# A hybrid attention and state-space layer on one core: one gate product moved into the states, the second FFN's opening reordered, head projections in two banks

## The chip, the core and the metric

The kernel runs on one core of a Trainium2 chip, as one launch. The metric is the device time of that launch in microseconds (us). Five engines work side by side, each through its own list of instructions in order: TensorE (PE, matmuls and transposes), VectorE (DVE), ScalarE (ACT), GpSimd (POOL), and SyncE (SP), which here does nothing but issue transfers. They are held together by semaphores that the code writes out by hand. PSUM, where TensorE writes, has eight banks of 128 x 512 float32.

## The reference

```python
h = h + 0.5 * swiglu(rmsnorm(h, ffn1_norm), ffn1_w_gate, ffn1_w_up, ffn1_w_down)
n = rmsnorm(h, mix_norm)
z = n @ w_in          # c_q 256 | c_kv 128 | k_rope 32 | u 512 | g_attn 1024 | g_ssm 1024
q  = rmsnorm(c_q) @ w_uq ; kv = rmsnorm(c_kv) @ w_ukv        # 8 heads: 64 + 32 rotary, values 64
attn = softmax(q k^T / sqrt(96)) v                           # bidirectional
y = S5_forward(u) + S5_backward(u) + D * u                   # 32 groups of 16, 64 complex states
glu = gelu(y) @ w_glu + b_glu ; ssm = glu[:, :512] * sigmoid(glu[:, 512:])
h = h + (sigmoid(g_attn) * (attn @ w_o_attn) + sigmoid(g_ssm) * (ssm @ w_o_ssm)) @ w_out
h = h + 0.5 * swiglu(rmsnorm(h, ffn2_norm), ffn2_w_gate, ffn2_w_up, ffn2_w_down)
out = rmsnorm(h, final_norm)
```

There are 1,024 tokens, the model is 1,024 wide and each FFN 2,816; all inputs are float32.

## The kernel before, in words

**Three passes.** Every large product is made of float32 operands split in a high and a low part. `three_passes` (L46 to L50) issues high x high (L48), low x high (L49) and high x low (L50) into one bank. So each operand needs a high part (a cast, mostly on ACT) and a low part (raw minus high, on DVE or POOL) before its product can begin.

**Phases.** The kernel runs through phases: first FFN (to about 720 us), projections out of `w_in` (to 836), state-space part (837 to 1068), GLU (to about 1180), attention (to 1512), merge (to 1669), second FFN (to the end at 2354). Inside a phase each engine has one block of code, written in order by hand; there is no scheduler.

**State-space phase** (`ssm_phase`). PE turns `u` (32 transposes, L1628), then makes the state inputs: 16 quads of 8 matmuls (`states`, L1638), whose banks ACT empties with two copies each (L1673, L1674, semaphore `ec`). It then makes the products within a chunk, 8 quads of 4 matmuls (`within`, L1647), with a matrix M (called `ss_C_mat` in the profile, as is everything in that space) loaded from `kern_dram`. DVE adds them to `u` (L1728, `wadd`), where POOL had multiplied `u` by the diagonal D (L1714). DVE then scans 127 steps over the states (L1735 to L1739) while PE makes gate products: `side.gp.product(pe, n)`, 16 of them in two groups, 48 matmuls each, from a tile of `w_in` (`ga_raw`, two buffers), its high part on ACT (L156) and its low part on POOL (L164). `GATES_FIRST` of them stand ahead of the outputs of the scan. SP loads tile n+2 of the gates only when the low part of tile n is done, and it stands in SP's list behind the load of the output matrix `C_dram` (4 MB), which waits for the last `within`.

**GLU phase.** PE turns y (L1814), ACT and DVE split it in two (`gl_yT_hi`, `gl_yT_lo` L1849), eight half tiles counted by `s_lo`. `glu.product(pe, n)` multiplies by the GLU weights, whose low parts (`glu_lo`, L164) DVE makes in between.

**Attention phase.** For a block g of 128 queries PE turns the probabilities of block g-2 in two parts (`turn`, L2020), makes the scores of block g, and, in some blocks, part 0 or 1 of the values (`values`, L2039 and L2040, bank `pv_out` = 6), the turned inverses (`inverses`, L2029, bank `inv_out` = 7), and one of the four projections of the next head (`project(n, x)`: x = 0, 1 the two halves of the queries, 6 products; x = 2, 3 the keys, 3 products). Projections come in the blocks 0, 1, 4, 5 of a head, behind everything else of their block. For the values of a pair of blocks J, ACT copies the upper half out of bank 6 (`at_spread` L2120) and DVE adds the lower half (L2208, semaphore `sum`); DVE then multiplies by the inverses (`scale`). In before all projections of heads 1 to 7 use bank 7. DVE's rows of a block come in this order: low part of turn 0 (L2202), maximum of the scores (L2191), low part of turn 1 (L2202), the sum (L2208) and its product (L2213), then the projection's rotary or low parts (L2181, L2182 or L2184).

**Second FFN** (`ffn_phase` with `ahead`). The residual is in `rows` (8 row tiles). ACT and DVE turn it into `f_B_hi` and `f_B_lo`; DVE multiplies the rows by their statistics and gain in place (L1039) once the store of the unscaled row to `kept` has read it. The weights come as raw tiles (L789); ACT makes the high part (L918), DVE the low part (L1023). POOL adds up raw tiles (L1289) and rows (L1272 to L1277) for the checks' sums, which PE turns (L1303, `turn_sums`).

Of the kernel before, what the change touches and what calls it, by code (L numbers as in the profile page):

```python
# [17 lines left out]
ALU = mybir.AluOpType  # L18
# [14 lines left out]
P = 128  # L33
# [653 lines left out]
def ffn_phase(nc, tag, gain, w_gate, w_up, w_down, rows, ident, psum, hidden, residual, x=None, finish=None, tables=None, ahead=0, following=None):  # L687
# [10 lines left out]
    with Phase(nc) as ctx:  # L698
# [85 lines left out]
        def _(sp):  # L784
# [24 lines left out]
            if ahead:  # L809
                load_matrix(0)  # L810
            take(0)
            take(1)
            sp.dma_start(gb[:], gain.rearrange("(a d) -> a d", a=1).broadcast_to([P, D])).then_inc(s_gain, 16)
# [4 lines left out]
            for m in range(QUAD, ST):  # L818
                take(m)
# [206 lines left out]
        def _(dve):  # L1026
# [57 lines left out]
            if ahead:  # L1084
                normalised(2)
# [6 lines left out]
            lows_low(3)  # L1092
            normalised(3)
# [489 lines left out]
def ssm_phase(nc, w, rows, rows_at, ident, psum, nT_hi, nT_lo, u, gates, kern_dram, C_dram, lam8_dram):  # L1583
# [5 lines left out]
    with Phase(nc) as ctx:  # L1589
# [18 lines left out]
        @block.sync  # L1608
        def _(sp):
            for t in range(T):  # L1610
                at = (T - 1 - t) * SG
                sp.dma_start(M[t * SG:(t + 1) * SG], kern_dram[:, :, at:at + P]).then_inc(s["m"], 16)
            sp.dma_start(Db, w["ssm_d"][0:1, :].rearrange("a (g i) -> a g i", i=SG).broadcast_to([P, GROUPS, SG])).then_inc(s["d"], 16)
            side.gp.load(sp, 0)
            side.gp.load(sp, 1)
            sp.dma_start(lam8[:].rearrange("p a b g -> p (a b g)"), lam8_dram).then_inc(s["lam"], 16)
            sp.wait_ge(s["within"], NQ)
            sp.wait_ge(s["ud"], NQ)
            sp.dma_start(C_mat[:], C_dram.rearrange("c p g x -> p c g x")).then_inc(s["c"], 16)
            side.sync(sp)  # L1620

        @block.tensor
        def _(pe):
# [16 lines left out]
            for q in range(2 * NQ):  # L1640
                states(q)
            pe.wait_ge(s["m"], 16 * T)
            for q in range(NQ):
                if q >= 4:
                    pe.wait_ge(s["wadd"], q - 3)
                for g in range(4 * q, 4 * q + 4):
                    mm = pe.matmul(psum[:, q % 4, g % 4 * P:(g % 4 + 1) * P], UT[:, g, :], M[:, g, :], start=True, stop=True)  # L1647
                mm.then_inc(s["within"], 1)
            pe.wait_ge(s["wadd"], NQ)
            for n in range(GATES_FIRST):  # L1650
                side.gp.product(pe, n)
# [16 lines left out]
        def _(act):  # L1668
# [9 lines left out]
            side.gp.high(act, 1)  # L1678
            for q in range(NQ, 2 * NQ):
                state(q)  # L1680

# [26 lines left out]
        @block.gpsimd  # L1708
        def _(pool):
            pool.wait_ge(s["d"], 16)  # L1710
            for q in range(NQ):
                pool.wait_ge(s["ut"], q + 1)
                g = slice(4 * q, 4 * q + 4)
                pool.tensor_tensor(u[:, g], u[:, g], Db[:, g].unsqueeze(2).broadcast_to([P, 4, T, SG]), ALU.mult).then_inc(s["ud"], 1)  # L1714
            for n in range(side.N):
                side.gp.low(pool, n)

        @block.vector
        def _(dve):
# [4 lines left out]
            for q in range(NQ):  # L1724
# [3 lines left out]
                dve.tensor_tensor(u[:, g], psum[:, q % 4, :].rearrange("p (g t i) -> p g t i", g=4, i=SG), u[:, g], ALU.add).then_inc(s["wadd"], 1)  # L1728
# [38 lines left out]
def glu_phase(nc, w, ident, psum, y, gates, partial):  # L1767

    with Phase(nc) as ctx:
# [38 lines left out]
        def _(pe):  # L1808
# [7 lines left out]
            pe.wait_ge(s_lo, NT)  # L1816
            for n in range(glu.N):
                glu.product(pe, n)
# [57 lines left out]
def attention_phase(nc, w, ident, psum, rows_at, latent_rows, trig_rows, aT_hi, aT_lo):  # L1876

    with Phase(nc) as ctx:
# [42 lines left out]
        job_bank = lambda n, x: psum[:, x if n == 0 else 7, :]  # L1921
# [46 lines left out]
        def _(pe):  # L1968
# [6 lines left out]
            def project(n, x):  # L1975
# [9 lines left out]
                elif n:  # L1985
                    pe.wait_ge(s["proj_act"], job)
                    pe.wait_ge(s["proj_dve"], job)
                    if n >= 2 and x in (0, 2):
                        pe.wait_ge(s["scale"], 2 * n - 3 + x // 2)
# [42 lines left out]
            def values(J, part):  # L2032

                if part == 0:
                    pe.wait_ge(s["tr_lo"], (4 * J + 4) * PARTS)
                    if J:
                        pe.wait_ge(s["sum"], J)
                for k in range(4 * part, 4 * part + 4):
# [491 lines left out]
```

## Time and profile before

| | |
|---|---|
| Median of three runs | 2366.19 us (2361.04 to 2367.4) |
| Profiled execution | 2355.74 us, its span 2354.0 us |
| Mean granted TensorE clock | 0.964 of full speed |
| PE busy | 2160.3 us (92% of the span) |
| DVE busy | 1489.9 us (63%) |
| ACT busy | 917.3 us (39%) |
| POOL busy | 592.3 us (25%) |
| Transfers | 263.52 MB, 112 GB/s over the span |

The span runs from the first to the last instruction of the core; the profiled execution lies 10.45 us under the median of the runs. Times inside a profile are us from the span's start.

### The profile page before, as it was taken

To read this page: it belongs to the slowest core of one execution; us is meant where nothing else is said; L and a number is where in the kernel's file an instruction comes from. 1 tells how busy PE (TensorE), PEld (TensorE's weight loads), DVE (VectorE), ACT (ScalarE), POOL (GpSimd) and SP (SyncE) were. 2 spreads that over 40 slices of the span, in tenths; PEclk is the share of its full clock that TensorE was granted. 3 is DMA by queue.
4 is the path that set the end of the run, shared out by engine and by line. 5 is a ranking of instruction groups with operands and counts; after the bars stand their busy time and mean duration, and the time that the engine had idled before them with its cause. 6 is when DMAs were issued, how large, how long until landed. Compare 5 with 4: busy or idle time off the path is not lost. (4 is left out here: it accounts for less than half of the span.)

```text
span 2354.0 us, 27672 instructions
## 1 busy us (share of the span) xinstructions
PE 2160.3 (92%) x10074; PEld 1789.2 (76%) x10074; DVE 1489.9 (63%) x2322; ACT 917.3 (39%) x1552; POOL 592.3 (25%) x494
## 2 busy tenths in 40 slices
PE   5999999999997979998959898699799999999997
PEld 4778888878886978886747776577678888887886
DVE  7786676657776229942357777462765655656777
ACT  5423333324453241153137776322333333223444
POOL 5347777810000022220012222000433333320000
PEclk8999999999998989998979999799899999999999
DMA  4424343376333264322420000163222324339433
GB/s 125 113 82 132 114 141 117 95 296 220 99 116 129 68 112 149 90 72 76 139 58 7 4 6 1 58 246 125 90 85 85 117 90 126 95 102 366 125 98 109
DMA packets 234615, 263.52 MB, mean 112 GB/s; under 512 B 34736, under 2 KB 169392, under 8 KB 233968
## 3 DMA queue, kind: packets, MB, share of 16 engines
q1 hardware_dynamic: 234480, 261.75, 35.0%
q8 instruction: 81, 1.33, 0.2%
q14 instruction: 54, 0.44, 0.1%
HBM read 185.13 MB, written 76.58 MB: 111 GB/s over the span
## 5 line engine op out<-in xcount | busy, mean ns | idle before, releaser
L48 PE MATMUL psum<-f_B_hi,f_A_hi 128*128 128x512 f32 x1232 | 487.1, 395 | 35.6 <-DVE f_B_lo L1051 22.7
L50 PE MATMUL psum<-f_B_hi,f_A_lo 128*128 128x512 f32 x1232 | 481.8, 391 | 0.0
L49 PE MATMUL psum<-f_B_lo,f_A_hi 128*128 128x512 f32 x1232 | 481.8, 391 | 0.0
L48 PEld LDWEIGHTS psum<-f_B_hi,f_A_hi 128*128 128x128 f32 x1232 | 232.8, 189 | 87.0 <-issue 30.1
L50 PEld LDWEIGHTS psum<-f_B_hi,f_A_lo 128*128 128x128 f32 x1232 | 232.6, 189 | 49.3
L49 PEld LDWEIGHTS psum<-f_B_lo,f_A_hi 128*128 128x128 f32 x1232 | 233.0, 189 | 47.0
L1289 POOL TENSOR_TENSOR f_S<-f_raw 128x512 f32<-128x512 f32 x88 | 131.0, 1489 | 470.4 <-DVE f_A_lo L1023 289.9
L918 ACT CAST f_A_hi<-f_S 128x512 fp32r<-128x512 f32 x176 | 109.3, 624 | 347.7 <-PE psum L50 339.7
L48 PE MATMUL psum<-f_wd,f_hh 128*128 128x512 f32 x616 | 240.6, 391 | 3.6 <-DVE f_wd L1068 3.6
L50 PE MATMUL psum<-f_wd,f_hh 128*128 128x512 f32 x616 | 240.3, 390 | 0.0
L49 PE MATMUL psum<-f_wd,f_hh 128*128 128x512 f32 x616 | 240.2, 390 | 0.0
L952 ACT CAST f_hh<-f_h_raw 128x512 fp32r<-128x512 f32 x154 | 96.0, 624 | 240.4 <-PE psum L50 231.7
L1023 DVE TENSOR_TENSOR f_A_lo<-f_raw,f_A_hi 128x512 fp32r<-128x512 f32 x132 | 135.3, 1026 | 68.0 <-ACT f_A_hi L918 67.3
L1066 DVE TENSOR_TENSOR f_hh<-f_h_raw,f_hh 128x512 fp32r<-128x512 f32 x154 | 106.5, 692 | 104.9 <-ACT f_hh L952 104.1
L1023 DVE TENSOR_TENSOR f_A_lo<-f_S,f_A_hi 128x512 fp32r<-128x512 f32 x176 | 140.1, 798 | 2.5 <-ACT f_A_hi L918 1.3
L48 PEld LDWEIGHTS psum<-f_wd,f_hh 128*128 128x128 f32 x616 | 116.0, 188 | 28.7 <-DVE f_wd L1068 4.4
L50 PEld LDWEIGHTS psum<-f_wd,f_hh 128*128 128x128 f32 x616 | 116.0, 188 | 24.2
L49 PEld LDWEIGHTS psum<-f_wd,f_hh 128*128 128x128 f32 x616 | 116.1, 188 | 23.9
L918 ACT CAST f_A_hi<-f_raw 128x512 fp32r<-128x512 f32 x132 | 81.8, 621 | 127.0 <-PE psum L50 127.0
L2202 DVE TENSOR_TENSOR at_PT_lo<-psum,at_PT_hi 128x512 fp32r<-128x512 f32 x128 | 87.8, 687 | 65.6 <-ACT at_PT_hi L2098 65.4
L1068 DVE TENSOR_TENSOR f_wd<-f_wd_raw,f_wd 128x512 fp32r<-128x512 f32 x154 | 105.7, 686 | 0.0
L1714 POOL TENSOR_TENSOR u<-u,ss_C_mat 128x512 f32<-128x512 f32 x8 | 9.8, 1268 | 375.4 <-DMA ss_C_mat<-ssm_d 375.4
(327 smaller groups left out, 4308.9 us busy)
## 6 DMA issues: line engine op xcount, KB each, us to landing
f_h_raw<-hidden SPq DMA_DIRECT2D x154, 256.0 KB, 2.7
hidden<-rows SPq DMA_DIRECT2D x44, 768.0 KB, 4.5
f_raw<-ffn_w_gate SPq DMA_DIRECT2D x44, 512.0 KB, 5.2
f_raw<-ffn_w_up SPq DMA_DIRECT2D x44, 512.0 KB, 5.1
f_wd_raw<-ffn_w_down SPq DMA_DIRECT2D x44, 512.0 KB, 9.1
rows<-x SPq DMA_DIRECT2D x16, 512.0 KB, 7.1
ga_raw<-w_in SPq DMA_DIRECT2D x16, 512.0 KB, 4.3
gates<-ga_sig SPq DMA_DIRECT2D x32, 256.0 KB, 2.2
```

The lines of the kernel that those rows point to most:

```text
L48: pe.matmul(out, lhs_hi, rhs_hi, start=first, stop=False, skip_group_check=go_on)
L49: pe.matmul(out, lhs_hi, rhs_lo, start=False, stop=False, skip_group_check=go_on)
L50: return pe.matmul(out, lhs_lo, rhs_hi, start=False, stop=last, skip_group_check=go_on)
L918: act.copy(A_hi[:, q], src).then_inc(s_hi, 1)
L952: act.copy(hh[v % 2][0][:], h_raw[v % 8][:]).then_inc(s_dhi, 1)
L1023: eng.tensor_tensor(A_lo[:, q], src, A_hi[:, q].bitcast(F32), ALU.subtract).then_inc(s_lo, 1)
L1066: dve.tensor_tensor(hh[v % 2][1][:], h_raw[v % 8][:], hh[v % 2][0][:].bitcast(F32), ALU.subtract).then_inc(s_dlo, 1)
L1068: dve.tensor_tensor(wd[v % 2][1][:], wd_of(q, k), wd[v % 2][0][:].bitcast(F32), ALU.subtract).then_inc(s_dlo, 1)
L1289: pool.tensor_tensor(S[:, i], a, b, op).then_inc(s_sum, 1)
L1714: pool.tensor_tensor(u[:, g], u[:, g], Db[:, g].unsqueeze(2).broadcast_to([P, 4, T, SG]), ALU.mult).then_inc(s["ud"], 1)
L2202: dve.tensor_tensor(pt(PT_lo, g, x), turned_bank(x), pt(PT_hi, g, x).bitcast(F32), ALU.subtract).then_inc(s["tr_lo"], 1)
```

## The change

Four places are edited. **State-space:** the first gate product moves between the last `states` and the first `within`; the `within` products take banks 4 to 7 instead of 0 to 3; SP loads gate tile 0 and D ahead of M; ACT casts tile 1 only after all states; POOL makes the low part of tile 0 after six of its eight multiplications by D. **GLU:** the first product no longer waits for all eight low half tiles, but inside its passes for two more at each k. **Second FFN:** SP stores rows 4 and 5 before it loads the first gate tile, and DVE scales rows 4 and 5 only after the low parts of the first tile. **Attention:** the projections use bank 6 for x = 0, 2 and bank 7 for x = 1, 3; they wait for the emptying of the projection before the last one (`job - 1`) instead of the last; x = 0, 2 wait for `sum` (the bank of the values) where they waited for `scale`, x = 1, 3 for `scale`; and the values wait for projections that had to be waited for by the inverses alone.

```diff
@@ -806,16 +806,18 @@
                     sp.dma_start(residual[m * P:(m + 1) * P, :], rows[:, m, :]).then_inc(s_kept[m], 16)
-            if ahead:
-                load_matrix(0)
             take(0)
             take(1)
+            if ahead:
+                take(QUAD)
+                take(QUAD + 1)
+                load_matrix(0)
             sp.dma_start(gb[:], gain.rearrange("(a d) -> a d", a=1).broadcast_to([P, D])).then_inc(s_gain, 16)
...
                 load_matrix(0)
-            for m in range(QUAD, ST):
+            for m in range(QUAD + ahead // 2, ST):
                 take(m)
@@ -1082,7 +1084,8 @@
             if ahead:
-                normalised(2)
+                variance(2)
+                rstd(2)
             lows_low(1)
@@ -1090,6 +1093,9 @@
             lows_low(3)
+            if ahead:
+                scaled(QUAD)
+                scaled(QUAD + 1)
             normalised(3)
@@ -1607,11 +1613,11 @@
         def _(sp):
+            side.gp.load(sp, 0)
+            sp.dma_start(Db, w["ssm_d"][0:1, :].rearrange("a (g i) -> a g i", i=SG).broadcast_to([P, GROUPS, SG])).then_inc(s["d"], 16)
             for t in range(T):
...
                 sp.dma_start(M[t * SG:(t + 1) * SG], kern_dram[:, :, at:at + P]).then_inc(s["m"], 16)
-            sp.dma_start(Db, w["ssm_d"][0:1, :].rearrange("a (g i) -> a g i", i=SG).broadcast_to([P, GROUPS, SG])).then_inc(s["d"], 16)
-            side.gp.load(sp, 0)
             side.gp.load(sp, 1)
@@ -1639,15 +1645,18 @@
                 states(q)
+            side.gp.product(pe, 0)
             pe.wait_ge(s["m"], 16 * T)
             for q in range(NQ):
-                if q >= 4:
+                if q < 4:
+                    pe.wait_ge(s["ec"], 2 * (2 * NQ - 3 + q))
+                else:
                     pe.wait_ge(s["wadd"], q - 3)
                 for g in range(4 * q, 4 * q + 4):
-                    mm = pe.matmul(psum[:, q % 4, g % 4 * P:(g % 4 + 1) * P], UT[:, g, :], M[:, g, :], start=True, stop=True)
+                    mm = pe.matmul(psum[:, 4 + q % 4, g % 4 * P:(g % 4 + 1) * P], UT[:, g, :], M[:, g, :], start=True, stop=True)
                 mm.then_inc(s["within"], 1)
             pe.wait_ge(s["wadd"], NQ)
-            for n in range(GATES_FIRST):
+            for n in range(1, GATES_FIRST):
                 side.gp.product(pe, n)
@@ -1675,9 +1684,9 @@
             side.gp.high(act, 0)
-            side.gp.high(act, 1)
             for q in range(NQ, 2 * NQ):
                 state(q)
+            side.gp.high(act, 1)

@@ -1709,10 +1718,12 @@
             for q in range(NQ):
+                if q == NQ - 2:
+                    side.gp.low(pool, 0)
                 pool.wait_ge(s["ut"], q + 1)
...
                 pool.tensor_tensor(u[:, g], u[:, g], Db[:, g].unsqueeze(2).broadcast_to([P, 4, T, SG]), ALU.mult).then_inc(s["ud"], 1)
-            for n in range(side.N):
+            for n in range(1, side.N):
                 side.gp.low(pool, n)
@@ -1725,7 +1736,7 @@
                 dve.wait_ge(s["within"], q + 1)
-                dve.tensor_tensor(u[:, g], psum[:, q % 4, :].rearrange("p (g t i) -> p g t i", g=4, i=SG), u[:, g], ALU.add).then_inc(s["wadd"], 1)
+                dve.tensor_tensor(u[:, g], psum[:, 4 + q % 4, :].rearrange("p (g t i) -> p g t i", g=4, i=SG), u[:, g], ALU.add).then_inc(s["wadd"], 1)
             dve.wait_ge(s["lam"], 16)
@@ -1813,9 +1824,8 @@
                 mm.then_inc(s_t, 1)
-            pe.wait_ge(s_lo, NT)
             for n in range(glu.N):
-                glu.product(pe, n)
+                glu.product(pe, n, (lambda k: pe.wait_ge(s_lo, 2 * k + 2)) if n == 0 else None)
             for n in range(KT):
@@ -1918,7 +1928,7 @@
         v_bank = lambda m: psum[:, 4 + m % 4, :]
-        job_bank = lambda n, x: psum[:, x if n == 0 else 7, :]
+        job_bank = lambda n, x: psum[:, x if n == 0 else 6 + x % 2, :]
         inv_out = psum[0:VH, 7, :]
@@ -1983,9 +1993,11 @@
                 elif n:
-                    pe.wait_ge(s["proj_act"], job)
-                    pe.wait_ge(s["proj_dve"], job)
+                    pe.wait_ge(s["proj_act"], job - 1)
+                    pe.wait_ge(s["proj_dve"], job - 1)
                     if n >= 2 and x in (0, 2):
+                        pe.wait_ge(s["sum"], 2 * n - 3 + x // 2)
+                    if n >= 2 and x in (1, 3):
                         pe.wait_ge(s["scale"], 2 * n - 3 + x // 2)
@@ -2035,6 +2047,8 @@
                         pe.wait_ge(s["sum"], J)
+                    pe.wait_ge(s["proj_act"], min(2 * JOBS + 2 * J, HEADS * JOBS))
+                    pe.wait_ge(s["proj_dve"], min(2 * JOBS + 2 * J, HEADS * JOBS))
                 for k in range(4 * part, 4 * part + 4):
```

What this does to the order of the instructions is seen on three engines. First PE in the state-space phase, before: `u` turned, the states (L1638), the products within a chunk (L1647), and then the gates' first product.

```order
L1628 MATMUL psum<-ident,u 128x128 x32
L1638 MATMUL psum<-ss_UT,rows 128x128 x64
L1647 MATMUL psum<-ss_C_mat,ss_UT 128x128 x32
L48 MATMUL psum<-nT_hi,ga_hi 128x512
L49 MATMUL psum<-nT_lo,ga_hi 128x512
L50 MATMUL psum<-nT_hi,ga_lo 128x512
```

The same place of the changed kernel (the three gate rows come 16 times before L1656; L1634, L1644 and L1656 are before's L1628, L1638 and L1647).

```order
L1634 MATMUL psum<-ident,u 128x128 x32
L1644 MATMUL psum<-ss_UT,rows 128x128 x64
L48 MATMUL psum<-nT_hi,ga_hi 128x512
L49 MATMUL psum<-nT_lo,ga_hi 128x512
L50 MATMUL psum<-nT_hi,ga_lo 128x512
L1656 MATMUL psum<-ss_C_mat,ss_UT 128x128 x32
```

One gate product of 48 matmuls has moved ahead of the 32 matmuls within a chunk. On SP the loads of that phase stand in before in this order (M is `kern_dram`, D is `ssm_d`):

```order
L1612 DMA ss_C_mat<-kern_dram 16x32x128 x8
L1613 DMA ss_C_mat<-ssm_d 128x512
L148 DMA ga_raw<-w_in 128x8x128 x2
L1616 DMA ss_lam<-lam_dram 128x128
L1619 DMA ss_C_mat<-C_dram 128x2x4096
L148 DMA ga_raw<-w_in 128x8x128
L1558 DMA gates<-ga_sig 128x512 x2
```

And in the changed kernel:

```order
L148 DMA ga_raw<-w_in 128x8x128
L1617 DMA ss_C_mat<-ssm_d 128x512
L1620 DMA ss_C_mat<-kern_dram 16x32x128 x8
L148 DMA ga_raw<-w_in 128x8x128
L1622 DMA ss_lam<-lam_dram 128x128
L1625 DMA ss_C_mat<-C_dram 128x2x4096
L148 DMA ga_raw<-w_in 128x8x128
L1564 DMA gates<-ga_sig 128x512 x2
```

Gate tile 0 and D have moved to the front; gate tile 2 (the single load behind `C_dram`) has kept its place. Second, PE in the attention phase, with what each row waits for. The profile's names of semaphores are shared between phases: `f1_gain` is here the attention's `sum`, `f1_x_in2` its `scale`, `f1_x_in5` its `tr_lo`, and `tb_kr` and `tb_xt` are `proj_act` and `proj_dve`. Before, for x = 0, x = 1 and the first values behind them:

```order
L2020 MATMUL psum<-ident,at_prob 128x128 x3
L48 MATMUL psum<-at_lT_hi,at_w_hi 128x512 [waits tb_kr,f1_x_in2,tb_xt,tb_x]
...
L48 MATMUL psum<-at_lT_hi,at_w_hi 128x512 [waits tb_kr,tb_xt]
...
L2039 MATMUL psum<-at_PT_hi,at_V 128x512 [waits f1_gain,f1_x_in5]
```

And in the changed kernel:

```order
L2032 MATMUL psum<-ident,at_prob 128x128 x3
L48 MATMUL psum<-at_lT_hi,at_w_hi 128x512 [waits tb_kr,f1_gain,tb_xt,tb_x]
...
L48 MATMUL psum<-at_lT_hi,at_w_hi 128x512 [waits f1_x_in2,tb_kr,tb_xt]
...
L2053 MATMUL psum<-at_PT_hi,at_V 128x512 [waits tb_xt,tb_kr,f1_gain,f1_x_in5]
```

No instruction has moved; x = 0 waits for `sum` instead of `scale`, x = 1 has `scale` added, and the values wait for the projections' emptying too. Third, DVE at the start of the second FFN, before:

```order
L1039 SCALAR_TENSOR_TENSOR rows<-rows,f_stat,f_gb 128x1024 x2
L1051 TENSOR_TENSOR f_B_lo<-psum,f_B_hi 128x4x128 x2
L1023 TENSOR_TENSOR f_A_lo<-f_raw_16682,f_A_hi 128x512 x2
L1051 TENSOR_TENSOR f_B_lo<-psum,f_B_hi 128x4x128 x4
L359 TENSOR_SCALAR f_stat<-f_stat 128x2
```

In the changed kernel:

```order
L1053 TENSOR_TENSOR f_B_lo<-psum,f_B_hi 128x4x128 x2
L1025 TENSOR_TENSOR f_A_lo<-f_raw_16733,f_A_hi 128x512 x2
L1053 TENSOR_TENSOR f_B_lo<-psum,f_B_hi 128x4x128 x4
L1041 SCALAR_TENSOR_TENSOR rows<-rows,f_stat,f_gb 128x1024 x2
L359 TENSOR_SCALAR f_stat<-f_stat 128x2
```

The two scalings of rows 4 and 5 have moved behind all low parts of the first tile.

## Rows read from the trace of the kernel before

**Rows 1.** The page, part 1: busy us, share of span, instructions.

```profile
PE 2160.3 (92%) x10074; PEld 1789.2 (76%) x10074; DVE 1489.9 (63%) x2322; ACT 917.3 (39%) x1552; POOL 592.3 (25%) x494
```

**Rows 2.** Timeline, PE, 836 to 892: start, length, instructions [idle <-releaser].

```profile
865.48 5.50 PE L1638 MATMUL psum<-ss_UT,rows 128*128 128x128 f32 x32 [12.10 <-ACT ss_H L1674]
...
878.98 0.50 PE L48 MATMUL psum<-nT_hi,ga_hi 128*128 128x512 f32 x1 [0.85 <-DVE u L1728]
```

**Rows 3.** Timeline of ACT, then POOL; transfers, 837 to 900 (us to landing).

```profile
861.65 1.05 ACT L156 CAST ga_hi<-ga_raw 128x1024 fp32r<-128x1024 f32 x1 [9.49 <-DMA ga_raw<-w_in]
...
893.91 2.39 POOL L164 TENSOR_TENSOR ga_lo<-ga_raw,ga_hi 128x1024 fp32r<-128x1024 f32 x1 [19.52 <-ACT ga_hi L156]
...
ss_C_mat<-C_dram SPq DMA_DIRECT2D x1, 4096.0 KB, 13.1
```

**Rows 4.** Timeline of PE, then DVE, in the GLU phase.

```profile
1084.25 0.79 PE L48 MATMUL psum<-gl_yT_hi,glu_hi 128*128 128x512 f32 x1 [5.05 <-DVE gl_yT_lo L1849]
...
1082.16 2.03 DVE L1849 TENSOR_TENSOR gl_yT_lo<-psum,gl_yT_hi 128x512 fp32r<-128x512 f32 x2
```

**Rows 5.** Waits, 1235 to 1560: us in total, times, longest.

```profile
PE psum L2020 <- DVE at_PT_lo L2202: 20.5, 14, 3.7
...
PE psum L48 <- DVE at_qf L2182: 4.6, 6, 0.8
PE psum L48 <- DVE at_KT_lo L2184: 4.6, 6, 0.8
```

**Rows 6.** Timeline of PE, then DVE, one head of the attention.

```profile
1325.47 0.48 PE L48 MATMUL psum<-at_lT_hi,at_w_hi 128*128 128x512 f32 x1
...
1330.13 0.47 PE L48 MATMUL psum<-at_lT_hi,at_w_hi 128*128 128x512 f32 x1 [0.78 <-DVE at_qf L2182]
...
1333.85 0.48 PE L2039 MATMUL psum<-at_PT_hi,at_V 128*128 128x512 f32 x1
...
1342.49 0.47 PE L48 MATMUL psum<-at_lT_hi,at_w_hi 128*64 128x512 f32 x1
...
1348.76 0.63 PE L2020 MATMUL psum<-ident,at_prob 128*128 128x128 f32 x4 [1.47 <-DVE at_PT_lo L2202]
...
1327.05 0.67 DVE L2208 TENSOR_TENSOR at_spread<-psum,at_spread 64x512 f32<-64x512 f32 x1
...
1333.98 0.69 DVE L2182 SCALAR_TENSOR_TENSOR at_qf<-psum,at_trig 32x512 f32<-32x512 f32 x1
...
1344.17 0.67 DVE L2208 TENSOR_TENSOR at_spread<-psum,at_spread 64x512 f32<-64x512 f32 x1
```

**Rows 7.** Timeline of PE, DVE and POOL, start of the second FFN.

```profile
1691.45 0.77 PE L48 MATMUL psum<-f_B_hi,f_A_hi 128*128 128x512 f32 x1 [14.98 <-DVE f_B_lo L1051]
...
1680.70 3.64 DVE L1039 SCALAR_TENSOR_TENSOR rows<-rows,f_stat,f_gb 128x1024 f32<-128x1024 f32 x2 [3.36 <-DMA kept<-rows]
...
1685.47 3.44 DVE L1023 TENSOR_TENSOR f_A_lo<-f_raw,f_A_hi 128x512 fp32r<-128x512 f32 x2
...
1697.74 0.69 DVE L1023 TENSOR_TENSOR f_A_lo<-f_raw,f_A_hi 128x512 fp32r<-128x512 f32 x1
...
1683.23 2.25 POOL L1272 TENSOR_TENSOR f_T_A_lo<-rows 128x512 f32<-128x512 f32 x1
```

**Rows 8.** Timeline of PE: stalls of 2.2 to 2.65 us elsewhere.

```profile
54.98 0.50 PE L48 MATMUL psum<-f_B_hi,f_A_hi 128*128 128x512 f32 x1 [2.65 <-DVE f_A_lo L1023]
...
1671.12 5.34 PE L1303 MATMUL psum<-ident,rows 128*128 128x128 f32 x32 [2.20 <-PEq L63]
...
1715.78 0.79 PE L48 MATMUL psum<-f_B_hi,f_A_hi 128*128 128x512 f32 x1 [2.65 <-DVE f_A_lo L1023]
```

**Rows 9.** Windows: us, then busy (count) of five engines, PEclk, DMA share, GB/s.

```profile
879.00:890.00 11.00, 11.00 (x48) 9.09 (x49) 9.66 (x40) 0.00 (x0) 0.00 (x0) 1.00 0.98 391
1084.20:1094.90 10.70, 10.65 (x40) 8.53 (x41) 0.00 (x0) 1.62 (x2) 0.00 (x0) 0.85 0.04 10
1671.20:1672.20 1.00, 1.00 (x5) 1.00 (x6) 0.00 (x0) 0.00 (x0) 0.00 (x0) 0.50 0.07 13
```


## The prediction

> **What bounds the kernel now.** I read the page first, then the timeline of PE around each edited place, then what DVE, ACT and POOL did there. PE is busy 92% of the span [rows 1] and the edits add or remove no matmul, so the change is worth what it does to PE's stalls and, through them, to PE's clock. Before, the edited places hold these stalls: 12.10 us in the states, for ACT [rows 2], which itself stood 9.49 us for the first gate tile's load because that was queued behind M [rows 3]; 5.05 us ahead of the first GLU product [rows 4]; 14.98 us at the start of the second FFN [rows 7]; and in each head of the attention 0.77 us at x = 1 and 0.77 at x = 3, which wait for the emptying of the one bank (4.6 us over 6 heads each [rows 5]), and 1.47 us at a turn just after x = 3, six times the same [rows 6]. That is 3.0 us of stalls a head: PE bounds the heads too.
>
> **State-space.** Gate tile 0 now comes first, so ACT casts it right behind its first eight quads (it was free from 861.65 - 9.49 = 852.2) and PE's states end near 859.7 instead of 870.98: ACT's eight last quads no longer wait for the tile. PE then has the product of 48 matmuls, which took 11.0 us [rows 9], to fill the time until M has landed and POOL's multiplications are done. Their place is where the stall of 12.1 us was. `within` then begins at 870.6 as before (it took the 8.0 us from 870.98 to 878.98 with DVE's last addition [rows 2]), so `C_dram`'s load and the scan are issued when they were. What follows is one product shorter: product 1 starts at 878.98 and ends at 889.9. Here is what is late next. Tile 2's load has kept its place behind the 4 MB of `C_dram`, which took 13.1 us to land, and its low part ended at 893.91 + 2.39 = 896.3 [rows 3]; nothing in that chain moves. Before, product 2 had its turn only at 900.8 and hid it. Now PE waits 6.4 us for it, and comes back at the low clock: 40 matmuls after the 5.05 us stall took 10.70 us at a mean granted clock of 0.85, where 48 took 11.0 at 1.00 [rows 9], so 1.5 us are lost. Sum: 11.0 removed, 6.4 + 1.5 + about 0.2 added, **-2.9 us**. The bounds: -1 if tile 0 or the first multiplications come some 2 us late, -7 if tile 2's load were not held by `C_dram` (then the end of the scan limits). The products behind have tiles that were loaded during the scan. The move of banks 0 to 3 to 4 to 7 costs nothing: ACT works on the states until some 2 to 4 us after PE's last one, and `within` comes 11 us after it.
>
> **GLU.** The last two low half tiles end at 1082.16 + 2.03 = 1084.2, and all 24 matmuls of the product stand behind them [rows 4]. Now only the last quarter does, 6 matmuls. The first 18 fit in the stall: 18 x 0.229 = 4.1 us of the 5.05. PE's pauses become under 1 us, so the 1.5 us of low clock [rows 9] go too: **-5.6 us**, between -4.1 (the clock falls all the same) and -5.6.
>
> **Second FFN.** DVE's chain ahead of the first product is: two scalings 1680.70 to 1684.34, two low parts of B to 1685.5, two low parts of A in 3.44 us, four more of B [rows 7]. The 3.64 us of scalings leave the chain. But the raw tile now queues behind two stores of 512 KB and lands some 3 us later, so POOL's work moves over DVE's. That matters because L1023 took 1.72 us each while POOL worked and 0.69 at 1697.74, when it was idle [rows 7]. I take the contention to stay: product 0 starts at 1686.9 instead of 1691.45, 4.6 us earlier; without it 1684.8, 6.6 earlier.
>
> The Trainium skill ("SBUF — State Buffer", section "SBUF: two separate sides") says that a DVE operation with two SBUF inputs and a GpSimd operation that reads SBUF exclude each other for a whole instruction, while operations with a PSUM input are spared. By that rule the two low parts of A stay slow as long as POOL has work, which is the 1686.9 that I use; the trace agrees (1.72 against 0.69 us).
>
> Not all of the 4.6 us reach the end. POOL's combination of the rows (from 1683.23 [rows 7]) starts some 5 us later, since rows 4 and 5 are scaled later, and PE's transposes of these sums stand in PE's order; they were hidden, and then come late. I take **-3.0 us**; the bounds are 0 (all given back) and -6.6.
>
> **Attention.** This is the large term. The instructions keep their order; x = 0 and x = 2 now wait for `sum`. By the code, that sum is DVE's row L2208 of the same block: behind the low part of turn 1, which is behind ACT's cast of a turn that PE issued directly ahead of the projection. Before, PE began x = 0 at 1325.47, and L2208 ended at 1327.05 + 0.67 = 1327.72; x = 2 at 1342.49 against 1344.84 [rows 6]. With 0.14 us from the sum's end to PE's start, the new stalls are 2.39 and 2.49 us: 4.88 a head. They are a chain of latency that starts with PE's own turn (cast, low part, sum), so a late PE does not find them done. Only heads 2 to 7 have the wait: 6 x 4.88 = 29.3 us.
>
> What comes back: at most every old stall of a head, 0.77 + 0.77 + 1.47 = 3.0, or 18 us in all; then +11 us is the floor of this term. I do not expect all. For x = 0, 1: +2.39, minus the 0.78 that x = 1 waited; but the values now wait for the emptying of x = 1, and DVE's L2182 for it ended at 1334.67, 0.8 us after the values began at 1333.85 [rows 6]. So +2.4. For x = 2, 3: +2.49, minus 0.77, minus half of the 1.47 at the turn (its low part is late by the same lateness as PE's turn ahead of it, except for what DVE had in its backlog): +0.9. Together 3.3 a head, **+19.8 us** with the clock unhurt. The top without clock is +29.3.
>
> The clock: at 1671.12, behind a stall of 2.20 us, the granted clock was 0.50 [rows 8, 9], which is the level of 1.2 GHz; behind 2.65 us at 1715.78 the first matmul took 0.79 us, behind the same 2.65 at 54.98 it took 0.50 [rows 8]. So a stall of this length brought the clock down in two cases of three, and none of the six stalls of 1.47 did. Twelve new stalls, eight falls; each costs 1.5 us of PE work as above, of which a third goes into later waits: 1.1 (my estimate), **+8.8 us**. Bounds 0 and 12 x 1.5 = +18. Attention: +28.6, from +11 to +47.
>
> **Sum.** -2.9 - 5.6 - 3.0 + 28.6 = +17.1. On the profiled execution, 2355.74 + 17.1 = 2372.8. That execution lies 10.45 us under the median of the runs (2366.19), so I put the forecast at 2366.19 + 17.1 = **2383 us**. A measurement of this kernel can tell some 0.3%, 7.1 us, from no change.
>
> **The rivals.**
> 1. *The forecast*: the `sum` stalls stand and are partly recovered, with some or most of the clock falls; +8 to +27 us. 0.62.
> 2. *All old stalls are recovered and the clock stays*: +11 in the attention, net 11 - 11.5, about 0; 2366. For it: the values and the turn at 1348.76 have slack only once PE is later, and 1.47 us did not harm the clock. Against it: the values' new wait for x = 1. 0.17, together with cases near it.
> 3. *Every stall brings the clock down, and little is recovered*: -11.5 + 29.3 + 18 = +36, 2402. It decides if a stall of 2.2 us is always enough, as at 1671.12. 0.12. A tile 2 that comes yet later, since M's loads now start later, would lead the same way.
> 4. *The other side, faster*: DVE's L2208 done when PE comes to the projection. It must end 2.3 us earlier in each head, which needs a turn's cast and low part that do not hang on PE's turn directly ahead. Then the attention loses its 9.2 us of waits at x = 1, 3, and the sum is -9.2 - 11.5 = -21, 2345. Against it is the code's order on DVE. 0.04. A milder form, the gains of the other edits at their bounds (-7, -5.6, -6.6 = -19) against the floor of +11, gives -8: 0.05 for both edges of it.
> 5. *The attention edit does nothing*, since other waits of PE already cover `sum`: then -11.5, 2355. The start of x = 0 without any stall in before speaks against it; it is counted in the 0.09 of rival 4.
>
> **How the numbers follow.** Rival 3 reaches to +36, rival 2 from about 0. Leaving out the top half of 3 and the faster cases, the range is 2366 to 2399. Faster by over 0.3%: 0.08. Within: rival 2 and the lower edge of the forecast, 0.19. Slower: 0.73.
>
> **What the changed profile would show.** PE: one gate product from about 859.7 to 870.6 and a stall of about 6.4 us near 890, released by the low part of tile 2; the first GLU product some 5 us earlier, with clock 1.00; product 0 of the second FFN 4 to 5 us earlier in its phase and a later wait for transposes of POOL's sums; in the attention six stalls at x = 0 and six at x = 2 of 2.3 to 2.5 us, released by DVE's sum, no stall at x = 1 and x = 3, each head 3 to 5 us longer, and granted clocks of 0.5 behind some of them. The prediction is wrong if a head grows by less than 1.2 us, if the stalls at x = 0, 2 are under 1 us, or if the stall near 890 is absent.

## The result and the profile after

| | before | changed |
|---|---|---|
| Median | 2361.04 us (15 runs, 2357.12 to 2370.03) | 2372.01 us (15 runs, 2367.79 to 2376.02) |
| Ratio to before, 95% interval | | 1.0042 [1.0033, 1.0051] |
| The same kernel in a later group of runs | 2361.18 us (17 runs) | 2375.94 us (5 runs), 1.0058 [1.0044, 1.0071] |
| Profiled execution's span | 2354.0 us | 2368.9 us |

The changed kernel is slower by 10 to 14 us. I had forecast +17 on a base of 2366.19, the median of three runs; fifteen runs put before at 2361.04, so 5 of the 11 us between 2383 and 2372 come from the base. The two profiled spans differ by 14.9 us, 4 us more than the medians: before's profiled execution (2355.74) lies 5.3 us under its median of fifteen, the changed kernel's (2370.71) only 1.3 us under its own. The first row of PE in each phase splits the spans. The columns of runs give the length of the phase in us in the kernel named; the last one is what I had forecast for changed minus before:

| phase | before | changed | attention edit alone | other three parts | forecast of the difference |
|---|---|---|---|---|---|
| state-space | 234.6 | 232.9 | 235.2 | 233.1 | -2.9 |
| GLU, to its first product | 12.1 | 7.0 | 12.1 | 7.0 | -5.6 |
| attention | 338.6 | 360.0 | 362.2 | 340.8 | +28.6 |
| second FFN, to its first product | 20.3 | 14.9 | 20.4 | 15.0 | -4.6 of it |
| second FFN, the rest | 662.5 | 668.1 | 662.6 | 669.0 | +1.6 of it |

The stretches between these phases differ by 0.1 us or less. So the attention edit costs, as forecast but less, and the second FFN gives its whole gain back. Busy time of PE grew by 9 us with the same 10,074 instructions [rows 1]; 7 of them lie in the attention phase, where the granted clock fell behind four of the new stalls. The page, part 1, of the changed kernel:

```profile
PE 2169.1 (92%) x10074; PEld 1793.7 (76%) x10074; DVE 1492.1 (63%) x2322; ACT 919.2 (39%) x1552; POOL 593.8 (25%) x494
```

PE's timeline in the state-space phase of the changed kernel, and the chain of product 2: POOL's low part, SP's stores of the gates, and the transfer of `C_dram` (us to landing).

```profile
854.53 1.70 PE L1644 MATMUL psum<-ss_UT,rows 128*128 128x128 f32 x10 [1.12 <-ACT ss_H L1683]
...
878.24 0.50 PE L48 MATMUL psum<-nT_hi,ga_hi 128*128 128x512 f32 x1 [0.85 <-DVE u L1739]
...
897.59 0.80 PE L48 MATMUL psum<-nT_hi,ga_hi 128*128 128x512 f32 x1 [8.17 <-POOL ga_lo L164]
```

```profile
895.20 2.35 POOL L164 TENSOR_TENSOR ga_lo<-ga_raw,ga_hi 128x1024 fp32r<-128x1024 f32 x1 [27.34 <-ACT ga_hi L156]
...
878.34 9.76 SPq L1564 DMA_DIRECT2D gates<-ga_sig  x2
...
ss_C_mat<-C_dram SPq DMA_DIRECT2D x1, 4096.0 KB, 15.1
```

The stall of 12.10 us in the states [rows 2] is 1.12 us, and product 1 begins at 878.24 where product 0 began at 878.98. But PE then waits 8.17 us for tile 2's low part. I had forecast 6.4. The low part ended at 897.55 instead of 896.3, since `C_dram`, ahead of the tile's load, took 15.1 us to land where it took 13.1 [rows 3]; and product 1 ended half a us earlier than I had put it. SP's stores of product 0, which in before were issued at 890.84, just ahead of `C_dram`'s landing, are now issued at 878.34, right behind it. All runs bear this out: `C_dram` took 14.0 to 15.1 us in the five profiles with the stores there, and 12.7 to 13.1 us in the eight with the stores later.

The only stall of PE inside the first GLU product of the changed kernel, against the 5.05 us of [rows 4]. The product's first matmul, at 1077.52, took 0.50 us where it took 0.79:

```profile
1083.03 0.50 PE L48 MATMUL psum<-gl_yT_hi,glu_hi 128*128 128x512 f32 x1 [0.99 <-DVE gl_yT_lo L1859]
```

One head of the attention, PE, then the two rows of DVE that the first stall waits for, then PE's waits for DVE from 1250 to 1460 (us in total, times, longest), and two windows (the third number from the end is the granted clock):

```profile
1328.78 0.47 PE L48 MATMUL psum<-at_lT_hi,at_w_hi 128*128 128x512 f32 x1 [2.16 <-DVE at_spread L2222]
...
1337.15 0.47 PE L2053 MATMUL psum<-at_PT_hi,at_V 128*128 128x512 f32 x1 [0.72 <-DVE at_qf L2196]
...
1348.23 0.66 PE L48 MATMUL psum<-at_lT_hi,at_w_hi 128*64 128x512 f32 x1 [2.16 <-DVE at_spread L2222]
```

```profile
1327.36 0.68 DVE L2216 TENSOR_TENSOR at_PT_lo<-psum,at_PT_hi 128x512 fp32r<-128x512 f32 x1
1327.95 0.67 DVE L2222 TENSOR_TENSOR at_spread<-psum,at_spread 64x512 f32<-64x512 f32 x1
```

```profile
PE psum L48 <- DVE at_spread L2222: 23.9, 11, 2.3
...
PE psum L2053 <- DVE at_qf L2196: 3.6, 5, 0.7
PE psum L2032 <- DVE at_PT_lo L2216: 2.1, 5, 0.9
```

```profile
1329.80:1330.80 1.00, 1.00 (x8) 0.87 (x7) 0.00 (x0) 0.37 (x1) 0.00 (x0) 1.00 0.00 0
1349.30:1350.30 1.00, 1.00 (x7) 0.80 (x5) 0.00 (x0) 0.52 (x2) 0.00 (x0) 0.50 0.00 0
```

This is the forecast's picture: 2.16 us at x = 0 and at x = 2 (2.31 in one case), twelve in all, behind `sum` (L2222 is before's L2208), none at x = 1 and 3, and some 0.72 at the values, which wait for x = 1's rotary rows. The clock was 1.00 behind the stall at 1328.78 and 0.50 behind that at 1348.23, with the same 2.16 us before both.

What a fall of the clock costs is seen where the same 20 matmuls follow a stall with and without it, from x = 0 to x = 1:

```profile
1251.63 0.47 PE L48 MATMUL psum<-at_lT_hi,at_w_hi 128*128 128x512 f32 x1 [2.16 <-DVE at_spread L2222]
...
1256.88 0.48 PE L48 MATMUL psum<-at_lT_hi,at_w_hi 128*128 128x512 f32 x1
...
1332.41 0.48 PE L48 MATMUL psum<-at_lT_hi,at_w_hi 128*128 128x512 f32 x1
```

With the fall they took 5.25 us (from 1251.63), without it 3.63 (from 1328.78): 1.6 us. The next 68 matmuls, up to x = 2, took 15.1 us behind the fall and 15.8 to 16.1 without one, which reads as PE, being late, waiting less there. So a fall costs some 0.7 to 0.9 us in all. Heads in which the clock stayed at 1.00 took 37.8 and 37.3 us from one x = 0 to the next (1366.71, 1404.51, 1441.81), against 34.4 and 34.2 in before (1359.61, 1394.03, 1428.21): 3.3 us more a head.

The start of the second FFN in the changed kernel: PE, then DVE and POOL; and behind them the row of before's DVE for the same scaling pair (L1039 is L1041 now).

```profile
1700.83 0.76 PE L48 MATMUL psum<-f_B_hi,f_A_hi 128*128 128x512 f32 x1 [9.61 <-DVE f_B_lo L1053]
...
1715.01 0.63 PE L1309 MATMUL psum<-ident,rows 128*128 128x128 f32 x4 [3.50 <-DVE f_B_lo L1058]
```

```profile
1708.08 4.51 DVE L1041 SCALAR_TENSOR_TENSOR rows<-rows,f_stat,f_gb 128x1024 f32<-128x1024 f32 x2
1712.51 1.75 DVE L1025 TENSOR_TENSOR f_A_lo<-f_raw,f_A_hi 128x512 fp32r<-128x512 f32 x1
...
1709.24 2.27 POOL L1279 TENSOR_TENSOR f_T_A_hi<-rows 128x512 f32<-128x512 f32 x1
```

```profile
1695.34 2.48 DVE L1039 SCALAR_TENSOR_TENSOR rows<-rows,f_stat,f_gb 128x1024 f32<-128x1024 f32 x2
```

The first product begins 14.9 us into the phase, 5.4 earlier than before. But 14 us later PE waits 3.50 us for DVE's low parts of the first sums, a stall that before does not have. DVE is late by its scaling of rows 6 and 7: 4.51 us, against 2.48 in before, when POOL stood idle; now POOL's sums of the rows stretch over it (2.27 us for one that takes 1.28 alone). Behind it, a low part of A took 1.75 us, against 0.69 [rows 7].

### The profile page after: what moved, and what is told of

Read it like the earlier page. It is cut to its first block and busy times, and to the rows that moved or that the text cites. A ratio compares the mean times of both kernels' runs of the same rounds, so it can differ in the third digit from the quotient of the medians.

```text
span 2368.9 us, 27690 instructions
## 1 busy us (share of the span) xinstructions
PE 2169.1 (92%) x10074; PEld 1793.7 (76%) x10074; DVE 1492.1 (63%) x2322; ACT 919.2 (39%) x1552; POOL 593.8 (25%) x494
## 5 line engine op out<-in xcount | busy, mean ns | idle before, releaser
L48 PE MATMUL psum<-nT_hi,ga_hi 128*128 128x512 f32 x256 | 101.0, 394 | 9.0 <-POOL ga_lo L164 8.2
```

The source lines that it names most:

```text
L48: pe.matmul(out, lhs_hi, rhs_hi, start=first, stop=False, skip_group_check=go_on)
```

## The experiments

Every kernel was timed in five rounds beside before. Four kernels are the change or parts of it, and seven change something besides.

**The attention edit alone.** Before with the diff of the attention phase as printed above, and nothing else.

> Before with only the attention edit. Theory A (the waits for the sum cost the time: 12 stalls of 2.16 us, 26 us, of which some 7 come back, and some clock falls): 16 to 22 us slower than before, ratio 1.007 to 1.009, and 12 PE stalls released by the sum in its trace. Theory B (the whole change is slow through something that the parts do to each other, such as later transfers, and the attention edit costs no more than its floor of 11 us): 11 us or less, ratio under 1.005.

Measured: 2381.9 us, ratio 1.0095 [1.008, 1.0111], +22 us; the attention phase took 362.2 us (+23.6), with twelve stalls of 2.16 to 2.31 us behind the sum. Theory A holds, at or just over the upper edge of what it gave (16 to 22 us); theory B falls. The granted clock 1.6 us behind these stalls was 0.50 after seven of the twelve; in the changed kernel's two profiles it was so after four and after three.

**The other three parts.** The whole diff without its attention hunks.

> The whole change without its attention edit. Theory A: -1.7 in the state-space phase, -5.2 in the GLU phase and 0 in the second FFN by the two profiles, so 5 to 8 us faster than before, ratio 0.997. As I predicted blind: -11.5 us, ratio 0.995. Theory B: about the same as before or slower.

Measured: 2352.98 us, ratio 0.9968 [0.9958, 0.9979], -7.5 us. The phases (table above) are those of the changed kernel, but for the attention, which is before's (338.6 to 341.9 us in the five profiles in which it is not edited). The parts add up to +15.

**The whole change again.**

> The whole change once more, on the chip and against the runs of before that this group shares. The attention edit alone was +22 us, the other three parts -7 us, together +15; the whole change had measured +10 against its own runs of before (ratio 1.0042). If the parts add up, the ratio here is 1.005 to 1.0065; if they interact, it stays at 1.0042 or lower and the attention phase of its trace is shorter than the attention edit's alone.

Measured: ratio 1.0058 [1.0044, 1.0071], +13.7 us. The parts add up within the intervals here; the first measurement's +9.9 is lower. The attention phase took 360.6 us. What makes the spread of some 4 us between groups is not settled. The number of clock falls differs from one execution to the next, but a fall is worth under 1 us here (362.2 with seven against 360.0 with four and 360.6 with three). Of the 7.1 us between this profile and the first of the changed kernel, 4.1 lie ahead of 837 us, where nothing is edited.

**The banks swapped.** The attention edit, with x = 0, 2 in bank 7 and x = 1, 3 in bank 6:

```diff
-        job_bank = lambda n, x: psum[:, x if n == 0 else 6 + x % 2, :]
+        job_bank = lambda n, x: psum[:, x if n == 0 else 7 - x % 2, :]
...
-                    if n >= 2 and x in (0, 2):
+                    if n >= 2 and x in (1, 3):
                         pe.wait_ge(s["sum"], 2 * n - 3 + x // 2)
-                    if n >= 2 and x in (1, 3):
+                    if n >= 2 and x in (0, 2):
                         pe.wait_ge(s["scale"], 2 * n - 3 + x // 2)
```

> Before with the attention edit, but x = 0, 2 in bank 7 (waiting for the scale) and x = 1, 3 in bank 6 (waiting for the sum, which stands a block earlier). The values' new waits stay. Theory A: no stall behind the sum, and those at x = 1, 3 and the turn behind x = 3 are gone or smaller, so 2 to 9 us faster than before (0.77 + 0.77 a head at x = 1, 3 is 9.2 us at most, the values' wait of 0.7 a head takes 4 of it). Theory B' (the values' wait for the projections, not the sum, is what costs): as slow as the attention edit alone, 10 us or more over before.

Measured: 2367.88 us, ratio 1.0036 [1.0022, 1.005], +8.5 us. The `sum` stalls are gone and with them 14 us of the 22, as theory A says. But I had expected it to be faster than before, and it is slower. Its waits of PE from 1250 to 1460, the stall of one head, and what ACT did ahead of that turn:

```profile
PE psum L2022 <- DVE at_PT_lo L2206: 17.5, 11, 2.4
...
PE psum L2043 <- DVE at_qf L2186: 4.3, 6, 0.7
```

```profile
1315.31 0.63 PE L2022 MATMUL psum<-ident,at_prob 128*128 128x128 f32 x4 [2.40 <-DVE at_PT_lo L2206]
```

```profile
1312.12 0.62 ACT L2130 CAST aT_hi<-at_att 64x512 fp32r<-64x512 f32 x1 [1.55 <-DVE at_att L2217]
1312.76 1.11 ACT L2111 ACTIVATE at_prob<-psum,at_nmx 128x1024 f32<-128x1024 f32 x1
```

The waits at x = 1 and 3 did not go away; they moved to the turn behind x = 3, which waits 2.40 us where it waited 1.47 [rows 6], and to the values. ACT's exponential for that turn stood behind its copy `aT_hi` (L2130), and that had waited 1.55 us for DVE's product, which stands behind the sum. So PE is ahead of a chain ACT, DVE, ACT, DVE that has its own length: cast, low part of turn 1, sum, product, `aT_hi`, exponential, cast, low part. PE without its bank wait only comes to it earlier. The stalls of 2.4 us also brought the clock down in some heads (0.65 and 0.50 in windows behind two of them), which the six of 1.47 us in before did not.

**The sum early.** The attention edit as it is, and on DVE:

```diff
                 if LAG <= g < G + LAG:
                     turned(g - LAG, 0)
+                if g and values_after(g - 1) and values_after(g - 1)[1] == 1:
+                    attended(values_after(g - 1)[0])
                 if g < G:
                     maximum(g)
                 if LAG <= g < G + LAG and PARTS == 2:
                     turned(g - LAG, 1)
-                if g and values_after(g - 1) and values_after(g - 1)[1] == 1:
-                    attended(values_after(g - 1)[0])
```

> Before with the attention edit and DVE's sum and its product moved ahead of the maximum and of turn 1's low part; PE's waits are those of the edit. Theory A (the stall is the latency of cast, low part and sum behind PE's own turn): the sum no longer hangs on that turn, the stalls at x = 0, 2 shrink from 2.16 to about 0.5 us, and the kernel is within 5 us of before. Theory C (DVE is simply full in these blocks, and the sum is late for want of DVE time): the stalls stay above 1.5 us or reappear in the same size at the next turn, since the maximum and the low part are late instead; 12 us or more over before.

Measured: 2350.77 us, ratio 0.9958 [0.9943, 0.9973], -9.9 us, 31 us faster than the attention edit alone.

```profile
PE psum L2022 <- DVE at_PT_lo L2206: 4.8, 9, 0.8
PE psum L2043 <- DVE at_qf L2186: 4.4, 6, 0.7
PE psum L48 <- DVE at_spread L2212: 4.1, 12, 0.6
```

The twelve stalls behind the sum hold 4.1 us in all (0.32 in most), where they were 26. With the sum taken out from behind that turn the stalls are gone, as theory A says: they were the latency of cast, low part and sum behind PE's own turn. Theory C falls; no stall of their size comes up later (0.8 us is the longest at a turn). That it would be faster than before was outside both theories.

**The order on DVE alone.** The same move on before, one bank and before's waits.

> Before with only DVE's sum and product ahead of the maximum and turn 1's low part: one bank, before's waits. It splits the 9.9 us that the sum-early kernel gained. If the two banks are worth something once the sum is there in time (the 0.77 us at x = 1 and x = 3), this is 3 to 9 us slower than the sum-early kernel, near before. If the two banks are worth nothing even then, and the order on DVE is the gain, this is as fast as the sum-early kernel, 8 to 12 us under before.

Measured: 2347.88 us, ratio 0.9943 [0.9929, 0.9957], -13.3 us; the attention phase took 324.7 us, against 338.6 and against 328.7 with the two banks.

```profile
PE psum L2020 <- DVE at_PT_lo L2202: 4.8, 13, 0.5
...
PE psum L48 <- DVE at_qf L2182: 4.3, 6, 0.8
```

The turn's six waits of 1.47 us (8.9) are thirteen short ones (4.8), those at x = 3 are gone, and those at x = 1 stay. The order on DVE is the whole gain. That the two banks take 3 us of it away is likely and not shown: the attention phase is 4 us longer with them, and they have the 4.1 us of waits for the sum besides, but the two intervals ([0.9929, 0.9957] and [0.9943, 0.9973]) overlap.

**Early and swapped.** Both of the edits above together.

> Before with the attention edit, banks swapped (x = 0, 2 in 7; x = 1, 3 in 6), and DVE's sum early. PE then waits for neither the sum nor the one bank. If DVE's time in these blocks is the limit behind PE (each wait removed on PE comes back at the next turn), the attention phase stays at or above the 324.7 us that the order on DVE alone gives with one bank. If the bank waits were true losses, it falls under 320 (0.7 us at x = 1, 3, less the values' 0.72).

Measured: 2346.16 us, ratio 0.9951 [0.9939, 0.9963]; attention phase 325.5 us.

```profile
PE psum L2022 <- DVE at_PT_lo L2206: 7.3, 18, 0.6
...
PE psum L2043 <- DVE at_qf L2186: 4.3, 6, 0.7
```

Not to be told from the order alone: 4.3 us of waits at x = 1 became 4.3 us at the values, which now wait for the same rotary rows of DVE. With every bank wait out of the way, the second bank is worth nothing that these runs can tell.

**Tile 2 first.** The state-space edit on before, and tile 2's load behind `lam8` instead of behind `C_dram`:

```diff
             sp.dma_start(lam8[:].rearrange("p a b g -> p (a b g)"), lam8_dram).then_inc(s["lam"], 16)
+            side.gp.load(sp, 2)
             sp.wait_ge(s["within"], NQ)
...
             if n + 2 < self.N:
-                self.gp.load(sp, n + 2)
+                if n:
+                    self.gp.load(sp, n + 2)
```

> Before with the state-space edit and gate tile 2 loaded ahead of the output matrix, nothing else. If the place of tile 2's load is what took back the gain: no stall of 8 us before product 2, the state-space phase 229 to 231 us where before has 234.6 to 236.3 and the edit as made 232.7 to 233.1, ratio 0.9975 or lower, 5 us or more. If something else held product 2, the phase stays at 233.

Measured: 2350.7 us, ratio 0.997 [0.996, 0.9979], -7.1 us; the phase took 228.7 us, 5.9 less than before and 4.2 less than with the edit as made. (One profile each; the profiles of the other kernels whose state-space phase is before's show 234.7 to 237.3 us for it, so the gains may be 1 to 2 us larger.)

```profile
878.75 0.50 PE L48 MATMUL psum<-nT_hi,ga_hi 128*128 128x512 f32 x1 [0.85 <-DVE u L1735]
...
1013.47 5.44 PE L1667 MATMUL psum<-ss_C_mat,rows 128*128 128x128 f32 x32 [3.87 <-ACT rows L1695]
```

There is no stall between 878.75 and 1013.47; what is left, 3.87 us, is the end of the scan and ACT's copy behind it. The place of tile 2's load took back some 4 us, over half of what the edit can give.

**The second FFN's order on DVE alone.** The edit without SP's part.

> Before with only the second FFN's edit on DVE (scaling of rows 4 and 5 behind the low parts); SP's order stays. Theory F (POOL's sums of rows move onto DVE's scaling of rows 6 and 7 and take back what the first product gained): the first product starts 4 to 7 us earlier, a new PE stall of 2 to 4 us stands behind the first sums' transposes, DVE's scaling pair for rows 6 and 7 takes 4 us or more where it took 2.48, and the total is within 2 us of before. Theory G (the stores put ahead of the first tile's load cost it): the first product starts as early, and the total is 3 us or more faster than before.

Measured: 2360.38 us, ratio 0.9996 [0.9985, 1.0006]. PE, then DVE's scaling pair:

```profile
1691.58 0.77 PE L48 MATMUL psum<-f_B_hi,f_A_hi 128*128 128x512 f32 x1 [9.07 <-DVE f_B_lo L1051]
...
1705.77 0.45 PE L1307 MATMUL psum<-ident,rows 128*128 128x128 f32 x1 [3.42 <-DVE f_B_lo L1056]
```

```profile
1698.85 4.50 DVE L1039 SCALAR_TENSOR_TENSOR rows<-rows,f_stat,f_gb 128x1024 f32<-128x1024 f32 x2
```

The first product starts 14.4 us into the phase, against 14.9 with SP's part too: SP's part costs that start half a us, and theory G, by which the total would be 3 us or more faster, falls. The stall of 3.42 us and the pair of 4.50 us are there: what theory F says.

**Rows 6 and 7 later.** The second FFN's edit, and `scaled(6)` and `scaled(7)` behind `sums_low(0)` instead of in front of `low(1, 0)`; `variance(3)` and `rstd(3)` stay.

> Before with the second FFN's edit and, besides, DVE's scaling of rows 6 and 7 moved behind the low parts of the next product's weights and of the first sums. Theory F (the PE stall of 3.5 us behind the first sums is DVE's scaling pair, held by POOL's sums): that stall shrinks to under 1 us and the second FFN is 3 us or more shorter than before's. If the loss is elsewhere (POOL's own chain of sums is the bound), PE waits at a later turn of sums and the phase stays at the same length.

Measured: 2358.96 us, ratio 1.001 [0.9998, 1.0022].

```profile
1690.73 0.77 PE L48 MATMUL psum<-f_B_hi,f_A_hi 128*128 128x512 f32 x1 [9.55 <-DVE f_B_lo L1053]
...
1703.54 0.66 PE L1315 MATMUL psum<-ident,f_T_A_hi 128*128 128x128 f32 x4 [0.42 <-POOL f_T_A_hi L1289]
...
1708.21 0.63 PE L1315 MATMUL psum<-ident,rows 128*128 128x128 f32 x4 [1.26 <-DVE f_B_lo L1058]
...
1711.24 0.66 PE L1315 MATMUL psum<-ident,f_T_A_lo 128*128 128x128 f32 x4 [0.60 <-POOL f_T_A_lo L1289]
```

The stall shrank from 3.50 to 1.26 us, not to under 1, and the second FFN is not 3 us shorter: it took 683.6 us, within the 682.7 to 685.2 of the profiles in which it is before's. Theory F names the first place where the gain goes and not the last. With DVE's pair out of the way PE waits 0.42 and 0.60 us for POOL's sums, whose chain begins only when row 4 is scaled, but this is 1 us of the 5.5 by which the first product starts earlier. From that product on, the same 140 or so matmuls took PE 34.3 us (1690.73 to 1725.05), against 29.7 in before (1691.45 to 1721.18): some 2 us of it are longer waits, the rest is a longer busy time of PE. So the last bound of this opening stays open; POOL's chain is a candidate that no run tests.

**A version faster than both.** State-space and GLU edits, tile 2 first, and the order on DVE; neither the attention edit nor the second FFN's.

> State-space and GLU edits, with gate tile 2 loaded ahead of the output matrix, and the order on DVE of the sum-early kernel, without the attention edit or the second FFN's. Against before: -5.1 for the GLU phase; in the state-space phase no stall of 8 us near 890, so -8 to -10 (limited by the scan's end) instead of -1.7; and what the order on DVE alone gives, 0 to -10. Sum 13 to 25 us under before. If the stall near 890 were set by something else than the place of tile 2's load, it stands as before, and the state-space phase stays at about 233 us.

Measured: 2333.45 us, ratio 0.9883 [0.987, 0.9897], -27.7 us, more than the 13 to 25 that I expected. Its phases: state-space 230.0 us, GLU to its first product 7.0, attention 324.2.

## Why the prediction went as it did

- **Direction and cause: right.** The attention edit's waits for `sum` are the loss, at the two places, for the reason and from the rows that were named. The faster rival (the sum done in time) did not come about in the change, and the sum-early kernel shows what it would have taken.
- **Size: too large, +17.1 against +9.9 and +13.7.** The step that failed is the clock: "Twelve new stalls, eight falls; each costs 1.5 us of PE work as above, of which a third goes into later waits: 1.1". Falls were 4 and 3 in the changed kernel's two profiles (7 with the attention edit alone). A fall cost 1.6 us of PE's work, as put, but half of it came back from later waits, so 0.7 to 0.9 us were left: some 2 to 4 us in all instead of 8.8. Two falls of three was taken from three stalls of 2.20 to 2.65 us in other phases. Against it the second FFN lost 3.0 us and the state-space phase 1.2 us of their forecast gains, and the base and the choice of executions make up the rest.
- **Attention without clock: nearly right.** I forecast 3.3 us a head; heads without a fall took 3.3 us more. The stalls show as 2.16 us, not 2.39 and 2.49, because I had counted from start to start, and the profile counts only the idle time behind the end of the last matmul. Counted as I did, x = 0 began 2.41 us late: its turn started at 1326.02, x = 0 follows such a turn by 0.35 us in before (1342.14 to 1342.49, at x = 2), and it started at 1328.78. Of the 18 us of old waits 5.7 were left in the window (3.6 at the values, 2.1 at turns). The phase grew by 21.4 us; less the clock's 2 to 4 that is 17 to 19, against my 19.8.
- **State-space: right in kind, -2.9 against -1.7.** The new stall was named, with its place; it was 8.17 us, not 6.4. "Nothing in that chain moves" was wrong: the stores of product 0 now go out right behind `C_dram`, and `C_dram` lands 2 us later.
- **GLU: -5.6 against -5.1.** Right.
- **Second FFN: -3.0 against 0.** The first product's start was right (-4.6 against -5.4). The failed step is "Not all of the 4.6 us reach the end ... I take -3.0": the phase gave all of it back. I had seen POOL's sums come later, but not that they then fall on DVE's scaling of rows 6 and 7 and stretch it from 2.48 to 4.51 us. But the pair is not the whole of it: with it moved away, the gain was still gone, and where the rest goes stays open. The rule of the Trainium skill ("SBUF — State Buffer", section "SBUF: two separate sides") that I weighed for the low parts of A bears on this pair too, which reads two SBUF operands; the trace agrees (4.51, 4.50 and, moved away, 3.12 us against 2.48).
- **Base.** 5 us of the forecast's distance come from the median of three. The difference itself is smaller in the medians (+11) than in the profiled executions (+15), which is nearer the forecast's +17.1 by the luck of which execution was profiled.
- **Rivals.** That every old stall is recovered (+11 in the attention) and that every stall brings the clock down (+47) were both wrong; the truth lay between them, nearer the first than I put it.

## What to carry to other kernels

A wait for a bank is worth removing only if the engine behind it has time: here every kernel with a second bank had x = 1's wait back at the next consumer of DVE's work (3.6 to 4.4 us in five of the six profiles, 1.7 in the sixth, which had the most falls of the clock), while moving two DVE rows ahead of two others, in one bank, gave 13 us. When a product is moved forward, look at what the next one needs and where its load stands in the queue; the load's place took back over half of this gain. And a step that makes one engine start earlier should be read for what it now runs beside: here DVE's scaling pair, its low part of A and POOL's sum took 1.8 to 2.5 times as long where they overlapped (4.51 us against 2.48, 1.75 against 0.69, 2.27 against 1.28).

## What the runs showed of the hardware that I had not expected

Stalls of the same length, 2.16 us, behind the same work, brought the granted clock to 0.50 in some heads and left it at 1.00 in others: 4, 3 and 7 of 12 in three profiles. The length of the stall alone does not decide it. And a 4 MB load landed 1 to 2 us later when 512 KB of stores were issued right behind it: in 14.0 to 15.1 us in five profiles, against 12.7 to 13.1 in the eight where these stores came 12 us or more after it. In the changed kernel PE paid for it, since it waited for the load behind both. In "Tile 2 first" (14.6 us) one tile's load stands beside the 4 MB, as in before, so that the stores are what was added. An estimate by the 391 GB/s of [rows 9] gives 1.3 us for 512 KB.
